# Prompt attention: the order of the eight query blocks of a head, and the score banks they use

## What is computed

```
s = (q_lat . c_kv + q_pe . k_pe) * SOFTMAX_SCALE        # per head, (queries, keys)
s = where(k_pos <= q_pos, s, NEG_INF)
p = softmax(s);  o = p @ c_kv                            # then  o @ w_uv @ w_o, summed over 8 heads
```

## Time and profile before

| | us |
|---|---|
| median of 3 runs (2489.29 to 2489.82) | 2489.8 |
| the profiled execution, its own time | 2489.48 |
| its span | 2487.7 |
| PE busy | 2401.2 (97% of the span) |
| DVE, ACT, POOL busy | 1085.0, 555.9, 725.4 |
| mean granted clock of TensorE | 0.989 of full speed |

### The profile page before, as it was taken

One profiled execution on the slowest core, in us unless ns is written; L12 is line 12 of the kernel. 1 busy time (PEld: TensorE's weight loads), 2 busy tenths in 40 slices (PEclk: granted clock), 3 DMA queues, 4 the chain that ended last, 5 costly groups with the idle time before them and its releaser, 6 DMA issues.

```text
span 2487.7 us, 36108 instructions
## 1 busy us (share of the span) xinstructions
PE 2401.2 (97%) x13411; PEld 2137.0 (86%) x13411; DVE 1085.0 (44%) x2021; ACT 555.9 (22%) x990; POOL 725.4 (29%) x472
## 2 busy tenths in 40 slices
PE   8999999999999989899999999989999999999996
PEld 8899999999999978488877786679999999999995
DVE  4443443344344362435444555443434433443446
ACT  3411111111111153232222234643111111111112
POOL 3532232232222270111111112653232322323235
PEclk9999999999999989999999999989999999999998
DMA  6111111111110110100000013412011111101111
GB/s 197 50 40 51 51 33 43 51 45 31 51 51 25 51 41 19 39 18 18 18 18 18 9 52 103 120 51 69 26 51 51 33 43 51 51 25 51 51 32 74
DMA packets 132609, 117.92 MB, mean 47 GB/s; under 512 B 9056, under 2 KB 119608, under 8 KB 132512
## 3 DMA queue, kind: packets, MB, share of 16 engines
q1 hardware_dynamic: 132528, 116.84, 15.3%
HBM read 110.95 MB, written 6.42 MB: 47 GB/s over the span
## 4 chain that ended last, share of the span: by engine, by line
PE 89%; DVE 4%; ACT 2%; issue 1%; DVEq 0%; POOL 0%; ACTq 0%
PE ps L728 23%; PE ps L729 23%; PE ps L730 23%; PE ps L1090 3%; PE ps L994 2%; PE ps L966 1%; PE ps L1077 1%; PE ps L1008 1%; PE ps L1140 1%; PE ps L999 1%; PE ps L1040 1%; PE ps L1035 1%; PE ps L1044 1%; PE ps L1043 1%; PE ps L1041 1%
## 5 line engine op out<-in xcount | busy, mean ns | idle before, releaser
L728 PE MATMUL ps<-XH,WGH 128*128 128x368 f32 (+1 forms) x2112 | 695.2, 329 | 4.9 <-DVE XL L1607 3.2
L729 PE MATMUL ps<-XL,WGH 128*128 128x368 f32 (+1 forms) x2112 | 695.7, 329 | 0.0
L730 PE MATMUL ps<-XH,WGL 128*128 128x368 f32 (+1 forms) x2112 | 693.5, 328 | 0.0
L1694 DVE TENSOR_TENSOR XR<-XR,ps 128x512 f32<-128x512 f32 x756 | 511.2, 685 | 8.7 <-PE ps L730 4.1
L1677 DVE TENSOR_TENSOR HF<-SG,ps 128x368 f32<-128x368 f32 x132 | 70.6, 535 | 907.3 <-PE ps L730 894.5
L728 PEld LDWEIGHTS ps<-XH,WGH 128*128 128x128 f32 x2112 | 397.3, 188 | 9.4 <-DVE XL L1607 3.9
L729 PEld LDWEIGHTS ps<-XL,WGH 128*128 128x128 f32 x2112 | 396.7, 188 | 1.8
L730 PEld LDWEIGHTS ps<-XH,WGL 128*128 128x128 f32 x2112 | 397.1, 188 | 0.0
L730 PE MATMUL ps<-WDH,HL 128*128 128x512 f32 (+1 forms) x792 | 313.6, 396 | 0.0
L729 PE MATMUL ps<-WDL,HH 128*128 128x512 f32 (+1 forms) x792 | 311.9, 394 | 0.0
L728 PE MATMUL ps<-WDH,HH 128*128 128x512 f32 (+1 forms) x792 | 310.8, 392 | 0.0
(11 more groups left out here) (234 smaller groups left out, 2997.9 us busy)
## 6 DMA issues: line engine op xcount, KB each, us to landing
RAWG<-ffn_w_gate SPq DMA_DIRECT2D x44, 512.0 KB, 6.0
RAWG<-ffn_w_up SPq DMA_DIRECT2D x44, 512.0 KB, 7.0
RAWD<-ffn_w_down SPq DMA_DIRECT2D x44, 512.0 KB, 3.4
CR<-cache_mla_l SPq DMA_DIRECT2D x64, 160.0 KB, 2.6
XR<-x_prompt SPq DMA_DIRECT2D x8, 512.0 KB, 12.1
WOR<-mla_w_o SPq DMA_DIRECT2D x8, 512.0 KB, 3.3
o_y_prompt<-XR SPq DMA_DIRECT2D x8, 512.0 KB, 2.6
WOA<-mla_w_o SPq DMA_DIRECT2D x7, 512.0 KB, 5.8
```

The source lines that it names most:

```text
L728: pe.matmul(out, w[0], x[0], start=start, stop=False)
L729: pe.matmul(out, w[0], x[1], start=False, stop=False)
L730: return pe.matmul(out, w[1], x[0], start=False, stop=stop)
L1694: dve.tensor_tensor(XR[0:r, t, ds], XR[0:r, t, ds], ps[0:r, 4 + 2 * w + half, :], ALU.add).then_inc(s_row[2 * l + 1], 1)
```

## The change

`ORDER` becomes 7, 0, 6, 1, 5, 2, 4, 3. No unit uses banks 6 and 7 any more. Up to 400 keys a unit uses bank 2 (`THIRD`); with 528 to 912 keys it uses the pair 0 and 1, half the keys in each (q = 3: 264 + 264); the unit of q = 7 uses the pair and, for its last 256 keys, bank 2. Side tiles alternate strictly between banks 6 and 7. So units that follow each other can now share banks: q = 4, then 3, then 7 of the next head all use the pair, and q = 7 and the q = 0 behind it share bank 2. `scores` therefore has new waits: for all exponentials of the unit before (pair after pair), or for the first of its two exponentials (bank 2 after q = 7), and the exponential of the 256 keys in bank 2 now runs first. The maxima and the exponentials of q = 3 become one instruction each in place of two (and the `min` and the sum that join the parts are gone). `NEXT_PLAN` puts both output tiles of a block together everywhere, and at positions 5, 6 and 7 ahead of the transposes (its first part).

```diff
--- before.py
+++ after.py
@@ -72,8 +72,8 @@
 LAST_DOWN = ((), (0, 1), (2, 3, 4, 5, 6, 7, 8))
 BANKS = 4
 FIRST_PLAN = [(1, 1, 0)] * 5 + [(0, 1, 0)] + [(0, 0, 0)] * 2
-NEXT_PLAN = ("-", "ab", "p"), ("pp", "a", "b"), ("p", "a", "b"), ("-", "ab", "pp"), ("p", "ab", "p"), \
-            ("p", "ab", "pp"), ("-", "a", "b"), ("-", "a", "b")
+NEXT_PLAN = (("", "ab", "p"), ("pp", "ab", ""), ("p", "ab", ""), ("p", "ab", "p"), ("p", "ab", "p"),
+             ("ab", "p", "pp"), ("ab", "", ""), ("ab", "", ""))
 ROPE_AFTER = (1, 3, 5)
 POOL_TILES = ((), (0,), (), (), (1,), (2,), (3,), (4, 5, 6, 7))
 PAGE_AFTER = (0, 1, 3, 5, 7, 8)
@@ -272,8 +272,8 @@
             sp.dma_start(GB[:, 1, :], a["ln_b"][k // 2, k % 2, :].partition_broadcast(P)).then_inc(s_gb, 16)
 
 
-        EXTRA = 6
-        ORDER = (7, 0, 6, 3, 5, 1, 4, 2)
+        THIRD = 2
+        ORDER = (7, 0, 6, 1, 5, 2, 4, 3)
         NQ = len(ORDER)
         UNITS = [(h, q) for h in range(H) for q in ORDER]
         NU = len(UNITS)
@@ -289,28 +289,24 @@
         def pieces(u):
 
             n = unit_q(UNITS[u][1])[2]
-            if u % 2 == 0:
-                if n <= 512:
-                    return [(0, 0, n)]
-                if n <= SEQ:
-                    return [(0, 0, n // 2), (1, n // 2, n)]
-                return [(0, 0, 512), (1, 512, n - 256), (EXTRA, n - 256, n)]
             if n <= 512:
-                return [(2, 0, n)]
-            return [(2, 0, n - 256), (EXTRA, n - 256, n)]
+                return [(THIRD, 0, n)]
+            if n <= SEQ:
+                return [(0, 0, n // 2), (1, n // 2, n)]
+            return [(0, 0, 512), (1, 512, n - 256), (THIRD, n - 256, n)]
 
         def extra(u):
 
-            return pieces(u)[-1][0] == EXTRA
+            return len(pieces(u)) == 3
 
         def main_scores(u):
 
             r, n = unit_q(UNITS[u][1])[1:]
             if extra(u):
-                return bank2(0, r, n - 256) if u % 2 == 0 else ps[0:r, 2, 0:n - 256]
+                return bank2(0, r, n - 256)
             if len(pieces(u)) == 2:
                 return ps[0:r, 0:2, 0:n // 2]
-            return ps[0:r, 0 if u % 2 == 0 else 2, 0:n]
+            return ps[0:r, THIRD, 0:n]
 
         def main_keys(u):
 
@@ -372,10 +368,7 @@
                                 made.append(("o", h_ - 1, 2 * q_ + "ab".index(c_)))
                     PLAN[-1].append(range(len(SIDE), len(SIDE) + len(made)))
                     SIDE += made
-                    later = range(u_, u_ + 2) if x_ == 0 else range(u_ + 1, u_ + 3)
-                    held = any(extra(e) for e in later if e < NU)
-                    for f_ in made:
-                        BANK.append(13 - EXTRA if held else 13 - BANK[-1] if BANK[-1] in (6, 7) else 6)
+                    BANK += [6 + f_ % 2 for f_ in range(len(BANK), len(SIDE))]
             assert not own
         LAST_SIDE = range(len(SIDE), len(SIDE) + 2 * (NT - 1))
         SIDE += output(H - 1)
@@ -1049,10 +1042,12 @@
                 if u % NQ == 0:
                     wait_projection(pe, h)
                     pe.wait_ge(h_ql, h + 1)
-                if extra(u) and u >= 2:
-                    before = [f for f in range(PLAN[u - 2][1].start) if BANK[f] == EXTRA]
-                    if before:
-                        wait_side(pe, before[-1])
+                if u >= 1:
+                    own, last = [p[0] for p in pieces(u)], [p[0] for p in pieces(u - 1)]
+                    if 0 in own and 0 in last:
+                        pe.wait_ge(h_ex, ex_count(u - 1))
+                    elif THIRD in own and THIRD in last:
+                        pe.wait_ge(h_ex, ex_count(u - 1) - 1)
                 for bank, lo, hi in pieces(u):
                     ins = score_piece(u, bank, lo, hi)
                 ins.then_inc(h_s, 1)
@@ -1429,14 +1424,14 @@
                 if u >= 2:
                     act.wait_ge(h_t, GROUP_AT[u - 1])
                 last = 2 if extra(u) else 0
+                if last:
+                    act.activation(PR[0:r, u % 2, n - 256:n], ps[0:r, THIRD, 0:256], ACT.Exp,
+                                   bias=MX[0:r, m, 2:3], accum_out=SM[0:r, m, 1:2]).then_inc(h_ex, 1)
                 out = PR[0:r, u % 2, 0:main_keys(u)]
                 if not extra(u) and len(pieces(u)) == 2:
                     out = out.rearrange("p (a b) -> p a b", a=2)
                 act.activation(out, main_scores(u), ACT.Exp, bias=MX[0:r, m, last:last + 1],
                                accum_out=SM[0:r, m, 0:1]).then_inc(h_ex, 1)
-                if last:
-                    act.activation(PR[0:r, u % 2, n - 256:n], ps[0:r, EXTRA, 0:256], ACT.Exp,
-                                   bias=MX[0:r, m, 2:3], accum_out=SM[0:r, m, 1:2]).then_inc(h_ex, 1)
 
             def output_rows(u):
                 m, r = u % (2 * NQ), unit_q(UNITS[u][1])[1]
@@ -1794,7 +1789,7 @@
                 dve.reduce_max(MX[0:r, m, 0:1], main_scores(u), AX_XY if split else AX_X, negate=True
                                ).then_inc(h_mx, 1)
                 if extra(u):
-                    dve.reduce_max(MX[:, m, 1:2], ps[:, EXTRA, 0:256], AX_X, negate=True).then_inc(h_mx, 1)
+                    dve.reduce_max(MX[:, m, 1:2], ps[:, THIRD, 0:256], AX_X, negate=True).then_inc(h_mx, 1)
                     dve.wait_ge(h_mx, mx_count(u) - 1)
                     dve.tensor_tensor(MX[:, m, 2:3], MX[:, m, 0:1], MX[:, m, 1:2], ALU.min).then_inc(h_mx, 1)
 
```

## The result

The changed kernel takes 2482.4 us (median of 7 runs, 2480.2 to 2483.9) against 2489.8 (median of the 7 runs beside it, 2489.1 to 2490.6); the ratio to the kernel before is 0.9966, with a 95% interval of 0.9956 to 0.9976, so 7.4 us less by the medians and 8.5 by the ratio. The profiled execution took 2483.87 with a span of 2482.1, the longest of the seven.

A forecast was written before the change was run, and what follows sets the result against it. TensorE was taken to bound the kernel. Terms: -14.4 (heads 1 to 6) + 2.2 (start) + 1.3 (clock) + 0.9 (head 0) + 1.0 (head 7) = -9.0 us, giving 2480.8 us; range 2476.0 to 2486.0.

The forecast's parts named there:

- What bounds it: Attention: TensorE's own time line bounds; work saved on DVE or ACT is worth nothing unless TensorE waits for it.
- Borrowed bank and alternation: Heads 1 to 6: q = 3's scores no longer wait for QTL, 1.13 us; alternating side banks removes about 2.0 per head.
- What comes back: Heads 1 to 6, waits on the tile before the last: 0.3 us at k0 and 0.3 at position 5.
- what goes: Heads 1 to 6: old waits of TensorE that disappear, 3.4 us per head.
- The five waits of the idle column: Each of heads 1 to 6: 2.6 us of idle time, about 0.17 more lost per wait, some 3.4 in all.
- The pair handed on: Scores of q = 3, 7 and 0 wait for exponentials; hidden in heads 1 to 6, so no cost there.
- only moved: Rival, heads 1 to 6: exposed score waits bring back up to 2.0 us per head; about 2487 to 2492; chance 0.11.
- Values of the last unit: Position 7, heads 1 to 6: values wait for OTL, 0.4 us lost against 0.3 before.
- The rival of a wait for PTS in every head: Head's last values wait for ACT's copy: 1.5 us lost per head, or slower than before, 2493; chance 0.05.
- The start: Unit 1's scores wait for unit 0's first exponential: pause of 3.7 us, first transposes 2.2 later, clock loss 1.3 besides.
- its clock term: Start of attention: the pause makes the granted clock fall to half, 1.3 us on, bounds 0 and 1.7.
- Head 0 and head 7: Head 0, without output tiles to cover waits, 0.9 us on; head 7, without projections, net 1.0 on.

The follow-up runs named there:

- one-bank run: Changed kernel with every side tile after the first eleven in bank 7, instead of alternating between banks 6 and 7: 2593.1 us, ratio 1.041.
- old table: Changed kernel with NEXT_PLAN of the kernel before, new unit order and banks kept: 2488.2 us, ratio 0.9993.
- second profile: Profile of the changed kernel run once more with no edit: 2482.7 us, ratio 0.9966.
- tile between scores and values: Changed kernel with, at positions 6 and 7, output tile a ahead of the transposes and b between scores and values: 2475.4 us, ratio 0.9934.
- best table: Changed kernel with unit 0's last 256 keys in bank 6 and another NEXT_PLAN separating tiles that would wait for each other: 2464.9 us, ratio 0.9899.
- the three other kernels that avoid it: Changed kernel with unit 0's last keys in bank 6 (2476.3); first query tile before unit 1's scores (2476.4); bank 6 plus output tile between scores and values (2472.9).

## Why the prediction was right

The time, 2480.8, is 1.6 under the median measured, inside the range. Attention as a whole came out at -9.3 against -9.0 in the profile, and against the profile again it is -11.1. Point by point:

- **What bounds it** held: all that moved is TensorE's own line.
- **Borrowed bank and alternation.** Right in kind; the one-bank run shows the mechanism at 16 us a head. What comes back is where and as large as forecast: about 0.3 at k0 and 0.25 at position 5, on the copy of the value tile two tiles back, as the prediction has it. With the 0.56 of the values that is 1.1, against 1.0, and the 1.2 measured against a head without waits. What was mis-sized is what goes: not 3.4 a head but 4.0 by the same measure. The five waits of the idle column, which the prediction counts, lost 3.6 from start to start. About 0.3 of the difference lies where the column shows nothing: before the change the two key tiles at position 3 took 2.53 to the next start, against 2.40 without a wait (the tile behind them waited for a copy that ended at 1270.60, and started at 1270.65), and the two value tiles at position 4 took 3.58 against twice 1.70, for a reason that is not shown. The heads gained 2.78, not 2.4, 2.3 us more over six.
- **The pair handed on.** No wait in heads 1 to 6, as worked out. The rival "only moved" fell for this kernel, but its mechanism is real: with the old table it took 1.3 idle a head. The prediction names the two output tiles ahead of the transposes as the cover, but has them in its sum as a loss at position 7 alone. Their worth is 1.3 a head, 57.38 against 56.04.
- **Values of the last unit.** 0.4 forecast, 0.56 lost. The values started 1.78 behind the transpose before the change, not 1.75. The rival of a wait for PTS in every head fell; it shows once, at the end of head 0 (below).
- **The start** was mis-sized in its clock term. The wait is as forecast: the scores start 0.62 after the exponential's start, and 6.27 after unit 0's first scores where it was 2.59, 3.7 on. The clock was given 1.3 with 1.7 as its bound, from one fall that lasted 3.4 us. It stayed low for 6.8 in the first profile, and the start cost 5.5; in the second 3.4, and 3.8. The bound was one instance of a thing that varies. At this place the clock fell around each pause of 3.5 us and more (six profiles), and not with the 1.05 and 1.3 that stand there in the others. The Trainium skill ("TensorE: Matmul & The Clock Gate", Why this matters for your kernels) says to keep idle gaps between bursts of matmuls short; by that rule, these traces agree. That the fall is avoidable at no cost was not seen.
- **Head 0 and head 7** came out as forecast, +0.9 and +1.1. In head 0 the scores of q = 3 and of q = 7 wait for exponentials where that was forecast, a little less than the 0.7 and 0.6 put down. Those of q = 0 do not wait (0.4 forecast), and the values at the end wait 0.52, for PTS:

```profile
1115.32 0.39 PE L1028 MATMUL ps<-KTH,QTH 128*128 128x264 f32 x1 [0.46 <-ACT PR L1433]
...
1119.95 0.47 PE L1028 MATMUL ps<-KTH,QTH 128*128 128x512 f32 x1 [0.44 <-ACT PR L1433]
...
1126.32 1.38 PE L1085 MATMUL ps<-VT,PTS 128*128 128x128 f32 x10 [0.52 <-ACT PTS L1237]
```

In the first profile the two errors, 2.3 too little gain in the heads and 2 too little loss at the start, cancel, and that is luck: it made the sum look better than its terms. In the second profile the start is only 0.3 off, and attention gained 11.1 in place of 9.0.

Two sums of the prediction do not follow from their terms. With its bounds for the three waits that come back, a head could gain 0.6 to 3.2, not 1.1 to 3.3, and the upper end of "only moved", 3 more than before, is 2493, not 2492. Neither enters the predicted time.

Left open: why the clock stays low for one stretch or for two; nothing was run on that.

## What to carry to other kernels

Read a wait from start to start, not from the idle column: here 0.89 in the column was 1.13 lost, 0.40 was 0.56, and a wait that the column leaves out lost 0.25. When buffers are handed from one user straight to the next, what counts is the work that lies between on the bounding engine: with the old table the handing-on took back 1.3 us a head, about as much as order and banks gained net. And where a new wait makes the matrix engine idle for several microseconds once, put any independent tile into the pause: it cost nothing and gave back 3.8 to 5.5 us by the traces, 6 by the medians.

## What the runs showed of the hardware

The pause at the start was 3.53 us long in five profiles. The granted clock was at its lower level for 6.8 us in four of them and for 3.4 in one; in a sixth profile, with a pause of 4.42, it was low for 6.8. The stretch ahead of attention, behind pauses of 2.36 and 1.28, varies in the same way without any change there: 3.4 us in ten profiles and 6.8 in that of the tile between scores and values, which is that kernel's slowest run.

This is also a part of the scatter outside attention. From 1600 to 1660 the mean granted clock was 0.86 in the first profile of the changed kernel and 0.89 in the second. That is about 1.8 us of work, as an estimate from these two numbers, and the stretch behind attention was 978.5 and 976.9 long. Whether it explains how far the runs of a kernel lie apart is not shown: without the pause at the start they lay within 1.6 us (best table), 2.2, 2.6 and 3.5 (the three other kernels that avoid it) and 4.3 (16 runs of the kernel before), with it within 3.7 and 5.7 (the two sets of the changed kernel).
